# Indexer scores: two heads' low-part pass on the two row halves of the array, and no scores for query tiles that keep every key

## What is computed

```python
def block(c):                                   # 64 queries
    dots = jnp.einsum('bqhd,bsd->bqhs', qib, ki) * (IDX_HD ** -0.5)     # 16 heads of width 64, one key
    score = jnp.einsum('bqh,bqhs->bqs', wib, jax.nn.relu(dots))
    admissible = key_chunk <= c                                         # chunks of 64 keys
    score = jnp.where(admissible[None, None, :], score, -jnp.inf)
    _, sel = lax.top_k(score, topk)                                     # topk = 256
    valid = admissible[sel]
```

## Time and profile before

| | |
|---|---|
| median of 3 runs | 2102.15 us (2100.63 to 2102.78) |
| the profiled execution | 2100.76 us, of which the span takes 2099.0 |
| TensorE busy | 1932.2 us, 92% of the span |
| VectorE, GpSimd, ScalarE busy | 1066.6, 687.1, 515.3 us |
| mean granted clock of TensorE | 0.945 of full |

### The profile page before, as it was taken

One profiled execution on the slowest core, in us unless ns is written; L12 is line 12 of the kernel. 1 busy time (PEld: TensorE's weight loads), 2 busy tenths in 40 slices (PEclk: granted clock), 3 DMA queues, 4 the chain that ended last, 5 costly groups with the idle time before them and its releaser, 6 DMA issues.

```text
span 2099.0 us, 29190 instructions
## 1 busy us (share of the span) xinstructions
PE 1932.2 (92%) x11545; PEld 1593.0 (76%) x11545; DVE 1066.6 (51%) x1785; ACT 515.3 (25%) x1042; POOL 687.1 (33%) x430
## 2 busy tenths in 40 slices
PE   6999999999978888888889877889999999999999
PEld 5887878788867778846667664678888888888887
DVE  4288889997866658454455323613231222321223
ACT  5366631112012222255411243310001000010000
POOL 4212133433333321045413310044334444344441
PEclk9999999999998887879999887989999999999999
DMA  7301011222210003000031100011111111121111
GB/s 226 83 21 31 21 41 51 71 91 81 81 62 2 2 2 121 12 1 1 1 121 41 50 21 0 10 57 44 50 40 60 50 41 49 40 60 50 48 42 80
DMA packets 111954, 102.45 MB, mean 49 GB/s; under 512 B 5051, under 2 KB 99310, under 8 KB 111598
## 3 DMA queue, kind: packets, MB, share of 16 engines
q1 hardware_dynamic: 109550, 92.68, 14.4%
q10 hardware_dynamic: 2304, 8.39, 1.0%
HBM read 87.42 MB, written 13.63 MB: 48 GB/s over the span
## 4 chain that ended last, share of the span: by engine, by line
PE 75%; DVE 13%; issue 5%; ACT 3%; POOL 3%; DMA 1%; DVEq 0%; POOLq 0%; ACTq 0%
PE ps L1182 8%; PE ps L1183 8%; PE ps L1184 8%; PE ps L386 5%; PE ps L387 5%; PE ps L388 5%; PE ps L360 5%; PE ps L362 5%; PE ps L361 5%; DVE top L1569 3%; PE ps L846 3%; DVE cacc L1584 2%; DVE score L1573 2%; PE ps L940 2%; PE ps L1077 2%
## 5 line engine op out<-in xcount | busy, mean ns | idle before, releaser
L654 POOL TENSOR_TENSOR WS<-WR,zero 128x1024 fp32r<-128x1024 f32 (+1 forms) x119 | 229.1, 1925 | 1060.2 <-PE ps L362 406.6
L656 POOL TENSOR_TENSOR WS<-WR,WS 128x1024 fp32r<-128x1024 f32 (+1 forms) x119 | 294.9, 2478 | 9.3
L1182 PE MATMUL ps<-HS,WS 128*128 128x512 f32 x704 | 275.2, 391 | 6.0 <-POOL WS L656 6.0
L1183 PE MATMUL ps<-HS,WS 128*128 128x512 f32 x704 | 274.9, 390 | 0.0
L1184 PE MATMUL ps<-HS,WS 128*128 128x512 f32 x704 | 274.8, 390 | 0.0
L401 DVE TENSOR_TENSOR X<-X,ps 128x512 f32<-128x512 f32 x272 | 184.6, 687 | 170.8 <-PE ps L388 167.2
L360 PE MATMUL ps<-HS,WS 128*128 128x512 f32 (+1 forms) x656 | 261.1, 398 | 8.7 <-ACT raw L1283 3.9
L362 PE MATMUL ps<-HS,WS 128*128 128x512 f32 (+1 forms) x656 | 257.7, 393 | 0.0
L361 PE MATMUL ps<-HS,WS 128*128 128x512 f32 (+1 forms) x656 | 257.6, 393 | 0.0
L1850 DVE TENSOR_TENSOR prod<-sil,ps 128x512 f32<-128x512 f32 x44 | 30.3, 688 | 407.5 <-PE ps L1184 407.5
L1573 DVE MATCH_REPLACE8 score<-top,score 128x1024 f32<-128x1024 f32 (+2 forms) x192 | 166.8, 876 | 0.0
(11 more groups left out here) (267 smaller groups left out, 2916.8 us busy)
## 6 DMA issues: line engine op xcount, KB each, us to landing
WR<-in_w_gu SPq DMA_DIRECT2D x44, 512.0 KB, 3.8
WR<-in_w_in SPq DMA_DIRECT2D x36, 512.0 KB, 3.7
WR<-in_w_down SPq DMA_DIRECT2D x22, 512.0 KB, 3.6
dsa_spill<-cacc ACTq DMA_DIRECT2D x12, 512.0 KB, 2.6
X<-in_x SPq DMA_DIRECT2D x4, 1024.0 KB, 9.3
KW<-in_w_xkv SPq DMA_DIRECT2D x8, 512.0 KB, 4.9
WR<-in_w_out SPq DMA_DIRECT2D x8, 512.0 KB, 3.6
X<-in_x SPq DMA_DIRECT2D x1, 4096.0 KB, 13.8
```

The lines of the kernel that those rows point to most:

```text
L654: pool.tensor_tensor(hi, w, bc(zero1[:, 0:1], [P, cols]), ALU.add).then_inc(w_hi, 1)
L656: pool.tensor_tensor(lo, w, hi.bitcast(F32), ALU.subtract).then_inc(w_split, 1)
L1182: pe.matmul(ps[:, b0 + half, :], lo, HS[:, 0, k, c], start=(k == 0), stop=False)
L1183: pe.matmul(ps[:, b0 + half, :], hi, HS[:, 1, k, c], start=False, stop=False)
```

## The change

The list of entries leaves out tiles 0 and 1 (10 pieces a head, 20 a pair, 160 in all), and is put in groups of four: head 0 with two pieces, then head 1 with the same two. One call of `dots` now makes a piece for both heads: the high pass of each over all 128 rows, as before, and then the low pass of each over the 64 rows that hold its high part, with the low key of the same rows. Hence the low query times the low key is no longer computed. The two heads' results go to banks two apart. There are ten calls a round, two in three of the places behind a triple, instead of 24.

TensorE waits before a call for the relu of the entry two back (`relu_out` at e - 1), and marks `dots_out` by 1 after a group's first call and by 3 after its second; ScalarE takes the group's first entry after the first call, and the other three after the second. VectorE's waits on its own additions follow the new order, and two of the eight memsets go.

```diff
-        entries = [(a, j, t, c, w) for a in range(8) for j in range(2) for t in range(TT)
-                   for c, w in chunks((t + 1) * P)]
-        PER_A = len(entries) // 8
-        PER_J = PER_A // 2
+        ranked = [(t, c, w) for t in range(TT) if (t + 1) * P > TOPK for c, w in chunks((t + 1) * P)]
+        assert len(ranked) % 2 == 0
+        entries = [(a, j) + ranked[i + q] for a in range(8) for i in range(0, len(ranked), 2)
+                   for j in range(2) for q in range(2)]
+        PER_A = 2 * len(ranked)
...
                 def dots(i):
-                    e = a * PER_A + i
-                    _, j, t, c, w = entries[e]
+
+                    e = a * PER_A + 4 * (i // 2) + i % 2
+                    _, _, t, c, w = entries[e]
                     if e >= 4:
-                        pe.wait_ge(relu_out, e - 3)
-                    for part in range(2):
-                        mm = pe.matmul(ps[:, 4 + e % 4, 0:w], qI[:, a % 2, j, t * P:(t + 1) * P],
-                                       kI[:, part, c:c + w], start=(part == 0), stop=(part == 1))
-                    mm.then_inc(dots_out, 1)
+                        pe.wait_ge(relu_out, e - 1)
+                    tok = slice(t * P, (t + 1) * P)
+                    for j in range(2):
+                        pe.matmul(ps[:, 4 + (e + 2 * j) % 4, 0:w], qI[:, a % 2, j, tok], kI[:, 0, c:c + w],
+                                  start=True, stop=False)
+                    for j in range(2):
+                        r = slice(SD * j, SD * (j + 1))
+                        mm = pe.matmul(ps[:, 4 + (e + 2 * j) % 4, 0:w], qI[r, a % 2, j, tok], kI[r, 1, c:c + w],
+                                       start=False, stop=True)
+                    mm.then_inc(dots_out, 3 if i % 2 else 1)
...
-                    for j in range(i * PER_A // steps_k, (i + 1) * PER_A // steps_k):
+                    for j in range(i * PER_A // 2 // steps_k, (i + 1) * PER_A // 2 // steps_k):
                         dots(j)
...
-                    act.wait_ge(dots_out, e + 1)
+                    act.wait_ge(dots_out, e + 1 if e % 4 == 0 else e // 4 * 4 + 4)
...
-                if e < PER_J:
+                if (a, j) == (0, 0):
                     dve.tensor_scalar(acc, relu[:, e % 3, 0:w], weight, None, ALU.mult).then_inc(acc_out, 1)
                 else:
-                    dve.wait_ge(acc_out, e + 1 - PER_J)
+                    dve.wait_ge(acc_out, e - 1 if j else e + 3 - PER_A)
...
-            for t in range(TT):
+            for t in range(2, TT):
                 clink(dve.memset(score[0:CHUNK, EOFF[t + 1] - CHUNK:EOFF[t + 1]], TAKEN))
```

## The result

The changed kernel is slower: 2122.5 us, the median of four runs (2120.22 to 2131.5), against 2102.13; ratio 1.0106, 95% interval 1.0075 to 1.0137. The forecast was 2105.8, and the range ended at 2118. The profiled execution took 2120.62 us, 19.9 more than the one before.

The account below looks back on a forecast made before the run. TensorE was taken to set the pace in key scoring, VectorE not far behind. Tiles -7.4, memsets -0.3, tiling +15.7, waits -5.1 and stage end +0.7 summed to +3.6 us: 2105.8 for a median, range 2092 to 2118.

Parts of the forecast that it names:

- The tiling: Key scoring, TensorE: each call changes tiling twice, 0.39 us, less what overlapping low pairs save; +1.96 a round, +15.7 us.
- The tiles left out: Key scoring: without tiles 0 and 1 TensorE has 0.92 us less work a round, -7.4 us over eight rounds.
- the term of the waits: Key scoring, TensorE's waits: losses fall from 6.5 us in all to 1.4, so -5.1 us, bounds -6.5 and +0.7.
- VectorE has the addition caught by the split until 3.4, one more until 4.1: Round's start, us from the unit's last triple: one addition held up beside GpSimd's split, the next done 0.7 later.
- The walk: Round's start, operation by operation over ScalarE and VectorE: fourth new relu done at 8.1, TensorE asks at 7.9, loses 0.2.
- The end of the stage: End of key scoring: three additions left, not two, the split catches the second; VectorE ends at 4.1, not 3.4: +0.7 us.
- The bound: TensorE's loss at a round's start was taken to lie between 0 and 1.03 us.
- The first catch: Round's start: the addition caught by the split ends 3.4 us after the last triple's start; TensorE loses 0.2 us a round.
- A relu comes too late in every group: Rival, key scoring: a relu is late by 0.2 us in 40 groups, 8 us, 2114; chance 0.05.
- The clock falls: Rival, key scoring: bubbles drop TensorE's clock at times, a mean of 0.9 costing 16 us, 2122; chance 0.05.

Follow-up runs that it names:

- reordered version: The changed kernel with the same matmuls in another order, both heads of one piece, then both heads of the next: 2102.07 us, ratio 0.9997.
- the second profile of the changed kernel: The changed kernel as it is, measured once more with more rounds: 2126.49 us, ratio 1.0122.
- late-split run: The changed kernel with GpSimd's split of eight units waiting until VectorE's last addition of the round, everything computed: 2117.26 us, ratio 1.0065.

## Why the prediction was wrong

**Right, by its own steps.** The tiling: 0.39 us a call, pairs that overlap in fp32r, +1.96 a round, measured +1.9. The tiles left out: -0.92 a round in TensorE's work; 19.74 - 18.95 = 0.79 with all waits away. The clock stayed at 1.00 in the profiled execution, though not in the second one. Together these put TensorE's bare work at +1.04 a round; it is 20.86 - 19.74 = +1.12.

**Wrong: the term of the waits**, and in it this step: "VectorE has the addition caught by the split until 3.4, one more until 4.1". The one more was caught as well. The walk had GpSimd's first operation as the only one in the way, because in the earlier trace rows the second lies beside the qI operations and hurts nobody. The change left three additions after the last call instead of two; the third now stood in the second operation's way. The term was -5.1 us, with +0.7 as its upper bound. Measured, the loss in a round rose from 1.1 to 3.0 us: +1.9 x 7, some +13, so the term was off by 18. The end of the stage, +0.7 forecast, pays the second catch once more: the last three additions end 6.5 us after the start of the round's last triple (281.46, 288.01), not 4.1. 18 and 2.4 are more than the 16.7 between forecast and result; the 3.3 us that are gone by the SwiGLU lie between.

The bound was the graver fault. 1.03, a loss already seen, was taken as the worst, though the prediction itself had moved one more operation of the caught kind behind the split. A bound from the rows had been at hand: one more caught addition, 2.4 us and not 0.65, in each of eight rounds, +14.

The first catch was undersized too, 0.2 for 0.9. With the low part's operation cut, where three additions are left and one is caught, as the walk had it, the caught one ends 3.8 us after the last triple's start and not 3.4: GpSimd starts 1.1 us behind that, and its first operation takes 2.14 us where the earlier trace rows has 1.90. Between the qI operations and the first new addition lie another 0.2 that the walk left out, and 0.1 more before the relu, so the fourth new relu is done at 8.8, not 8.1.

In the reordered version (one catch, qI beside the second operation) the loss is 21.07 - 20.86 = 0.2, and the stage takes 2.9 us more than in the kernel before; +3.6 was forecast. But two additions and not three are left there, so this agreement does not confirm the walk. The time, 2102.07 on a before of 2101.98, is that of no change.

**The rivals.** None named the mechanism. "A relu comes too late in every group" had the right queue, but in the middle of the round and without GpSimd. "The clock falls" was right in kind for the second profile of the changed kernel, where a stretch at 1.2 GHz adds some 1.5 us to each of three rounds; the first has the 23 us without it.

## What to carry to other kernels

Count what stands on an engine's queue when another engine's long operation starts, and ask of each whether it is of a kind that waits for it; an order that adds one operation there can cost more than the matmuls it rearranges. Price a change of the array's tiling by the excursion, there and back with the longer first matmul behind each change (0.39 us here), and take it only where it saves well above that: one pair of 512-column passes saves 0.22. When two changes come together, time the plain one alone; here leaving work out was worth 17 us, and its partner hid it.

## What the runs showed of the hardware

**Which VectorE operations GpSimd catches.** An addition (relu and score, both from SBUF) that started while a GpSimd tensor_tensor ran ended 0.55 us behind it: 2.2 to 2.9 us for 0.75. A convolution step (3.30 for 1.29) and a tensor_scalar (2.32 for 0.74) were held up likewise in the late-split run. An addition that was already running when GpSimd started was not held up (0.75, at 140.52). The qI operations, with one operand in PSUM, took 2.79 for four with and without it. Nor was MAX8 slowed in the late-split run: a pair takes 1.68 at 400.25, with GpSimd idle, and 1.68 at 403.56, beside GpSimd's operation of 402.34 and the start of that of 404.31. The Trainium skill ("SBUF — State Buffer", Who interferes with whom) states this split: VectorE with two SBUF inputs, or in a two-port mode, takes turns with a GpSimd instruction that reads SBUF, and the other is blocked for the whole instruction. The traces agree, with 2.88 against 0.75.

**Two additions in a row can be caught**, one by each of two GpSimd operations 0.08 us apart. The first catch ends at 143.57, when the second operation has been running since 143.10, and the next addition then ends at 146.38, 0.55 us behind that one.

**TensorE's clock** fell to 1.2 GHz for 3.4 us behind a round start with two waits, which lost 1.59 and 2.03 us. In the changed kernel, whose rounds lose 0.95 and 1.87 us in both its profiles, it fell in three rounds of one and in none of the other, so these losses alone do not settle whether it falls. In the kernel before, with one loss of 1.03 a round, the stage's clock stayed at 1.00. Each such stretch made its round some 1.5 us longer.
